# The recurrence's Q projection moves into the stage of half products of a one-layer decoder step

## What is computed

```python
h = rmsnorm(x, lp['norm_mix'])
z = h @ lp['w_in']                      # 1024 x (10*256 + 4*1024)
qa, ka, va, qb, fb, ib, gb, xc, gc, xd, gl = jnp.split(z, split_at, axis=-1)
...
log_f = jnp.logaddexp(jnp.log(lb), jnp.log1p(-lb) + jax.nn.log_sigmoid(fr))
kb = (1.0 - lb) * jax.nn.sigmoid(-fr)
qh = jax.nn.silu(qb.astype(F32))
o, S = gla_chunk_scan(to_h(qh), to_h(kb), to_h(ib.astype(F32)), to_h(log_f), S0.astype(F32), chunk)
o = rmsnorm(o, lp['hgrn_norm']).reshape(B, L, BRANCH_W) * jax.nn.silu(gb.astype(F32))
```

## Time and profile before

| | before |
|---|---|
| median of 3 runs | 1751.24 us |
| the profiled execution, its own time | 1751.34 us |
| its span in the profile | 1749.5 us |
| TensorE busy | 1723.3 us, 98% |
| VectorE, ScalarE, GpSimd busy | 65%, 42%, 45% |
| granted TensorE clock | 0.999 of full speed |
| DMA | 214.80 MB, 123 GB/s in the mean |

### The profile page before, as it was taken

The page is one execution under the profiler, slowest core; times in us unless marked ns, Lnnn a source line. Parts: engine busy times, 40 slices in busy tenths (PEclk is TensorE's granted clock), DMA queues, the critical chain, the costliest instruction groups (busy, mean ns, idle before and its releaser), DMA issues.

```text
span 1749.5 us, 30931 instructions
## 1 busy us (share of the span) xinstructions
PE 1723.3 (98%) x12865; PEld 1676.3 (96%) x12865; DVE 1140.7 (65%) x1275; ACT 733.4 (42%) x1038; POOL 781.6 (45%) x531
## 2 busy tenths in 40 slices
PE   8999999999999999999999999999999999999998
PEld 8999999998999977899999999999999999999998
DVE  6931115826774667657745877888888887775844
ACT  6433334443422556612335554444444443333521
POOL 1666773431222311212123476677776637668021
PEclk9999999999999999999999999999999999999999
DMA  6643226132221542456524222232222375334032
GB/s 229 76 124 117 99 75 215 37 101 81 67 82 68 196 118 67 159 195 236 209 74 148 86 87 105 101 120 99 99 99 99 117 287 209 117 118 148 26 128 95
DMA packets 84798, 214.80 MB, mean 123 GB/s; under 512 B 14866, under 2 KB 32050, under 8 KB 83506
## 3 DMA queue, kind: packets, MB, share of 16 engines
q1 hardware_dynamic: 73714, 189.48, 31.9%
q0 software_dynamic: 4032, 14.68, 2.7%
q10 hardware_dynamic: 6912, 8.65, 1.4%
HBM read 149.48 MB, written 63.40 MB: 122 GB/s over the span
## 4 chain that ended last, share of the span: by engine, by line
PE 91%; DVE 3%; ACT 2%; DMA 2%; issue 1%; POOL 0%; SPq 0%; DVEq 0%; ACTq 0%; POOLq 0%
PE ps L1656 24%; PE ps L1106 21%; PE ps L1704 10%; PE ps L1093 10%; PE ps L1236 10%; PE ps L1688 3%; PE ps L1324 2%; PE ps L1191 1%; DMA masks<-in_wb 1%; PE ps L1409 1%; PE ps L1133 1%; PE ps L1573 1%; PE ps L1443 1%; PE ps L1430 1%; PE ps L1741 1%
## 5 line engine op out<-in xcount | busy, mean ns | idle before, releaser
L3384 POOL TENSOR_TENSOR Wl<-BIG,Wh 128x512 fp32r<-128x512 f32 x110 | 144.0, 1318 | 115.3 <-ACT Wh L2211 115.3
L3241 POOL CAST Uh<-BIG 128x1024 fp32r<-128x1024 f32 x27 | 36.5, 1350 | 283.8 <-PE ps L1093 193.8
L3030 DVE SCALAR_TENSOR_TENSOR ps<-BIG,fpar,ps 128x1023 f32<-128x1023 f32 x84 | 107.9, 1285 | 36.1 <-ACT ps L2302 35.2
L1093 PE MATMUL ps<-Hh,Uh 128*128 128x352 f32 x384 | 127.2, 331 | 0.8 <-ACT BIG L1940 0.8
L2565 DVE TENSOR_TENSOR BIG<-BIG,ps 128x528 f32<-128x528 f32 x45 | 31.6, 704 | 144.2 <-PE ps L1236 143.9
L1093 PE MATMUL ps<-Hh,Ul 128*128 128x352 f32 x384 | 123.5, 322 | 0.0
L1093 PE MATMUL ps<-Hl,Uh 128*128 128x352 f32 x384 | 123.3, 321 | 0.0
L3336 POOL TENSOR_TENSOR Ul<-BIG,Uh 128x1024 fp32r<-128x1024 f32 x15 | 36.1, 2412 | 163.3 <-ACT Uh L2171 163.3
L1656 PE MATMUL ps<-Hl,Wh 128*128 128x264 f32 x528 | 107.1, 284 | 0.0
L3019 DVE TENSOR_TENSOR BIG<-BIG,ps 128x528 f32<-128x528 f32 x110 | 77.3, 703 | 42.8 <-PE ps L1656 36.9
L1704 PE MATMUL ps<-Sl,Vh 128*128 128x264 f32 x504 | 101.9, 283 | 0.0
(11 more groups left out here) (496 smaller groups left out, 5590.6 us busy)
## 6 DMA issues: line engine op xcount, KB each, us to landing
BIG<-in_wu SPq DMA_DIRECT2D x44, 512.0 KB, 4.6
hidden<-BIG SPq DMA_DIRECT2D x22, 528.0 KB, 2.7
late_gates<-BIG SPq DMA_DIRECT2D x18, 528.0 KB, 3.0
BIG<-sums SPq DMA_DIRECT2D x12, 792.0 KB, 4.9
BIG<-in_wgl SPq DMA_DIRECT2D x9, 1024.0 KB, 6.0
BIG<-in_wd SPq DMA_DIRECT2D x6, 1536.0 KB, 9.7
H<-late_gates SPq DMA_DIRECT2D x17, 528.0 KB, 4.4
gates<-BIG ACTq DMA_DIRECT2D x48, 176.0 KB, 1.9
```

What stands on the lines that cost most here:

```text
L1093: ins = nc.tensor.matmul(psb(fill_bank(p)), w[:, u % 2, k], x[:, k, part * PART:part * PART + PART], start=(k == 0 and w is Uh and x is Hh ...
L3030: link(v.scalar_tensor_tensor(y[:, back:SEQ], x[:, 0:SEQ - back], w, y[:, back:SEQ], ALU.mult, ALU.add), v.scalar_tensor_tensor(ys[:, :, b ...
L3384: nc.gpsimd.tensor_tensor(Wl[:, b], src, Wh[:, b].bitcast(F32), ALU.subtract).then_inc(S("w_lo"), 1)
```

## The change

The Q pair is no longer made by `block_z`. It becomes pair number 1 (`Z_PAIR`) of now 10 pairs: its raw weights come from the last two tiles of `wz` (`Z_COLS` has Q's columns last), its sums are made like a gate's, its two rows skip the sigmoid, go to `late_gates`, and SP loads them into `QB` later. `RING` and `USERS` lose QB0 and QB1. Behind the pairs come F, G, then V: FB0 and FB1 take the place of QB0 and QB1, GB0 and GB1 that of FB0 and FB1. TensorE puts the transposes of `turn` around VA0 and between VA0 and VA1. ScalarE's `before()` starts when groups 0 to 3 of the transposes are copied; it loads a table set first, and the copies of groups 4 to 11 and of VA0 and VA1 stand between its steps. The counts of semaphores and the index of a gate in `late_gates` follow. The diff, with one line around each edit:

```diff
@@ -66,7 +66,7 @@
 NORM_ORDER = (KA, KA + 1, QA, QA + 1)
-Z_COLS = (1792, 2304, 2048, 1280, 768, 1024, 1536, 512, 256, 0)
+Z_COLS = (1792, 2304, 2048, 1280, 1024, 1536, 512, 256, 0, 768)
@@ -132,8 +132,8 @@
          "gc_kept0": ("pages_in3", 0), "gc_kept1": ("s0_in", 0), "a_lo": ("vt_done", 12)}
-PAGES_FROM = (32, 80, 80, 32)
-SIG_FROM = (("pages_in0", 288), ("pages_in1", 336), ("pages_in2", 336), ("pages_in3", 288),
+PAGES_FROM = (48, 80, 96, 32)
+SIG_FROM = (("pages_in0", 304), ("pages_in1", 336), ("pages_in2", 352), ("pages_in3", 288),
             ("s0_in", 64), ("cd_in", 128), ("gate_stored0", 384), ("gate_stored1", 384))
@@ -183,9 +183,10 @@
 FILLS = QKS + UNITS
-ZB = 14
+ZB = 12
 COVER = 2
-PAIRS = (4 * LATE - COVER) // 2
+Z_PAIR = 1
+PAIRS = (4 * LATE - COVER) // 2 + 1
 SPLITS = ZB + FILLS
@@ -236,9 +237,9 @@
-USERS = ("XC0", "XC1", "XD0", "XD1", "GC0", "GC1", "IB0", "IB1", "C00", "C01", "QB0", "QB1", "C10", "C11", "FB0", "FB1",
-         "D0", "D1", "GB0", "GB1", "VA0", "VA1")
-RING = ("XD0", "XD1", "GC0", "GC1", "IB0", "IB1", "QB0", "QB1", "FB0", "FB1", "GB0", "GB1", "VA0", "VA1")
+USERS = ("XC0", "XC1", "XD0", "XD1", "GC0", "GC1", "IB0", "IB1", "C00", "C01", "FB0", "FB1", "C10", "C11", "GB0", "GB1",
+         "D0", "D1", "VA0", "VA1")
+RING = ("XD0", "XD1", "GC0", "GC1", "IB0", "IB1", "FB0", "FB1", "GB0", "GB1", "VA0", "VA1")
 FRONT = RING.index("IB1") + 1
@@ -684,7 +685,8 @@
             def pair_weights(c, sem):
-                src = a["wgl"].rearrange("i v p k m -> (i v) p k m")[COVER + 2 * c:COVER + 2 * c + 2]
+                first = COVER + 2 * (c - (c > Z_PAIR))
+                src = a["wz"][18:20] if c == Z_PAIR else a["wgl"].rearrange("i v p k m -> (i v) p k m")[first:first + 2]
                 sp.dma_start(gate_raw(c), src.rearrange("h p k m -> p h k m")).then_inc(on(sem), 16)
@@ -774,6 +776,9 @@
             rows_back(2, Z[:, GC:GC + 2, :], on("gw_in0"))
+            for half in range(2):
+                sp.wait_ge(*upto(f"g_stored{half}", 16 * (Z_PAIR + 1)))
+            sp.dma_start(QB, late_gates[2 * Z_PAIR:2 * Z_PAIR + 2].rearrange("i p t -> p i t")).then_inc(on("gw_first"), 16)
@@ -829,7 +834,8 @@
                 i, u = divmod(s, 8)
-                src = gates[i * EARLY + TURN_OF[u] + QKS] if u < EARLY else late_gates[i * LATE + u - EARLY - COVER]
+                n = i * LATE + u - EARLY - COVER
+                src = gates[i * EARLY + TURN_OF[u] + QKS] if u < EARLY else late_gates[n if n < 2 * Z_PAIR else n + 2]
                 sp.dma_start(gate_row(s), src).then_inc(S(gate_loaded(s)[0]), 16)
@@ -1250,19 +1256,21 @@
             for i in range(2):
-                block_z(f"QB{i}")
+                block_z(f"FB{i}")
             pe.wait_ge(S("cd_in"), 128)
...
             for i in range(2):
-                block_z(f"FB{i}")
+                block_z(f"GB{i}")
             for i in range(2):
                 unit(f"D{i}", wpool[:, i], Z[:, XD + i], 3 + i)
-            turned_v(0, turn[:, 0], range(2))
-            block_z("GB0", (0, lambda: turned_v(0, turn[:, 0], (2,))))
-            turned_v(1, turn[:, 1], range(2))
-            block_z("GB1", (0, lambda: turned_v(1, turn[:, 1], (2,))))
-            block_z("VA0")
+
+            def input_turned():
+                turned_v(0, turn[:, 0], (2,))
+                turned_v(1, turn[:, 1], (0,))
+            turned_v(0, turn[:, 0], (0, 1))
+            block_z("VA0", (0, input_turned))
+            turned_v(1, turn[:, 1], (1, 2))
             block_z("VA1")
@@ -1837,10 +1845,10 @@
-            def turned_v(n):
-
-                for g in range(3):
-                    m = 3 * n + g
+            def turned_out(ms):
+
+                for m in ms:
+                    n, g = divmod(m, 3)
                     act.wait_ge(S("vt_done"), m + 1)
@@ -1867,7 +1875,10 @@
                     act.wait_ge(*upto("g_copied", 2 * c + 2))
-                nc.scalar.activation(GY[:, half], GY[:, half], ACT.Sigmoid).then_inc(on("g_sig"), 1)
+                if c == Z_PAIR:
+                    act.sem_inc(on("g_sig"), 1)
+                else:
+                    nc.scalar.activation(GY[:, half], GY[:, half], ACT.Sigmoid).then_inc(on("g_sig"), 1)
@@ -1921,16 +1932,13 @@
                 for g in range(2):
-                    z_out(("QB", "FB")[i] + str(g), (QB, FB)[i][:, g])
+                    z_out(("FB", "GB")[i] + str(g), (FB, Z[:, GB:GB + 2, :])[i][:, g])
             for i in range(2):
...
             act.wait_ge(S("pool_read"), 2)
-            turned_v(0)
-            z_out("GB0", Z[:, GB, :])
-            turned_v(1)
-            z_out("GB1", Z[:, GB + 1, :])
+            turned_out(range(4))
@@ -1946,14 +1954,16 @@
                 f, q, g = FB[:, 0], QB[:, 0], Z[:, GB, :]
+                act.preload_act_table_set("natural_log_exp_and_others")
                 act.wait_ge(S("d_rows"), 16)
-                for user in ("FB0", "QB0", "GB0"):
+                for user in ("FB0", "GB0", "FB1", "GB1"):
                     z_wait(user)
-                for user in ("FB1", "QB1", "GB1"):
-                    z_wait(user)
+                act.wait_ge(*upto("gw_first", 48))
                 link(nc.scalar.activation(bE, f, ACT.Abs))
...
                 nc.scalar.activation(bE, bE, ACT.Ln, bias=1.0).then_inc(S("b_acts"), 1)
+                turned_out((4, 5))
+                z_out("VA0", turn[:, 0])
                 act.wait_ge(S("b_pre"), 1)
@@ -1963,8 +1973,11 @@
                 chunk_decays()
+                z_out("VA1", turn[:, 1])
+                turned_out((6, 7))
                 act.wait_ge(S("b_pre"), 5)
                 nc.scalar.activation(bE, bd_, ACT.Exp, scale=-1.0).then_inc(S("b_acts"), 1)
+                turned_out(range(8, 12))
@@ -2002,10 +2015,6 @@
                     before()
-                    for j in range(2):
-                        z_out(f"VA{j}", turn[:, j])
-                    for j in range(2):
-                        turned_v(2 + j)
                     act.wait_ge(S("c_rows"), 16)
@@ -2613,7 +2622,7 @@
-            dve.wait_ge(*upto("gw_in1", 80))
+            dve.wait_ge(*upto("gw_in1", 96))
             for i in range(2):
@@ -3240,7 +3249,7 @@
                 pool.wait_ge(S("w_hi"), r_ - 1)
-                if r_ == RING.index("QB1"):
+                if r_ == RING.index("FB1"):
                     pool.wait_ge(*upto("g_stored0", 16 * PAIRS))
```

## The result

The changed kernel takes 1758.37 us in the median (six runs, 1757.47 to 1760.88) against 1751.24 us for the kernel before (now six runs as well, 1749.55 to 1753.83). The ratio on record is 1.0037, with a 95% interval of 1.0026 to 1.0048; the two medians alone give 1.0041. It is slower by about 7 us, where 0.3 us less was forecast, and it lies above the range of 1748.4 to 1752.6. The profiled execution is 1755.7 us long, 6.2 us more than that of before.

The account below looks back on a forecast made before the run. It took TensorE, busy 98% of the span, as the bound: -2.79 us for the products and +2.5 us for later keys gave -0.3 us, 1750.9 us from a median of 1751.24, range 1748.4 to 1752.6.

Parts of the forecast that it names:

- The products and E: Front stage: a 20.58 us pair replaces 23.37 us of blocks, -2.79 us; E, the end of VA1, moves from 397.94 to 395.15.
- Movement through DRAM: Writes to `late_gates`, load into QB and weight loads stay hidden: nothing, with 0 to 0.1 us kept for more traffic.
- the order F, G, V: F, G, V instead of Q, F, G keeps block distances and the transposes' sum: nothing, at most 0.2 us either way.
- ScalarE's chain: Preparation under V, now behind D: spill lands in 6.0 us, first sigmoid at 386.8, eight small multiplications start at 395.1.
- The ports: After E, GpSimd's cast and subtraction hold VectorE's eight small multiplications; keys' transposes at 402.0, E + 6.8 against E + 4.33: +2.5 us.
- TensorE's other condition: All 12 groups of transposes must be copied, until E + 5.0; alone costs 0.7 us, covered by the 2.5 us for the keys.
- The sum: Whole kernel: -2.79 + 2.5 = -0.3 us, from the 1751.24 us median to 1750.9 us.
- the sum's term +2.5: Behind VA1: the keys' transposes start 2.5 us later after E, counted as 2.5 us of the kernel's time.
- a difference behind the state products: Sign of a wrong prediction: any difference arising behind the state products, where it counted none.
- the rivals: Preparation in time, 1749.1 (0.28); shuffle free, 1748.4 to 1747.7 (0.10); late spill, 1751.9 (0.12); pair's late data, 1 to 3 us (0.05).
- rival 3: Pooling rows' spill lands late, at 9.7 us; ScalarE's logs wait, keys end near 402.9: net +0.7 us, 1751.9; chance 0.12.
- The chance of 0.06 for a loss of over 0.2%: Whole kernel slower by over 0.2%, through the pair's weights or rows coming late or a spill landing over 12.5 us.

Follow-up runs that it names:

- experiment 1: Changed kernel with GpSimd's cast and subtraction of the tile behind V held until VectorE has made the keys; 1751.75 us, ratio 0.9996 to the kernel before.
- experiment 2: Changed kernel with 14 more products of 352 columns, used by nothing, where TensorE waits for the keys; 1753.97 us, ratio 1.0009 to the kernel before.
- experiment 6: Changed kernel with half a gate product (12 of 24 products) brought forward into the gap behind VA1, GpSimd's split not held; 1754.00 us, ratio 1.0011 to before.
- experiment 3: Kernel before, with one added wait so VectorE's eight small multiplications come only after VA1 is copied out of PSUM; 1760.06 us, ratio 1.0041.

## Why the prediction was wrong

**The products and E: right.** E came at 395.39, forecast 395.15; 0.20 of the 0.24 stood already at the first pair. A new wait of 0.4 us at FB0 for ScalarE replaced the 0.6 us that TensorE had lost to VectorE in the last pair.

**Movement through DRAM and the order F, G, V: right.** No wait in the changed profile goes back to the rows of Q. The spill landed later than at its 6.0 us, and ScalarE's logs began at 379.17, 1.7 us later than in my sum; that used up room that was there: 1.34 us were left, in which ScalarE idled behind the logs.

**ScalarE's chain: right.** The first sigmoid began at 386.83, forecast 386.8, and the eight multiplications at 395.17, forecast 395.1.

**The ports: right.** The hold of the small form, which no row had shown, is 5.32 us against 2.44 in experiment 1. The Trainium skill's rule ("SBUF — State Buffer", section "Who interferes with whom") and this case agree on it; that the eight run in a two-port mode is what the rule asks for, and no trace shows the mode. For operations with two SBUF inputs that section of the Trainium skill names only GpSimd instructions that read SBUF, which the prediction left out; GpSimd's two here read it. The keys' transposes began at 402.04 (forecast 402.0), released by VectorE's key multiplication, and the state products at 404.17 (forecast 404.0).

**TensorE's other condition: right.** The copies of the 12 groups were forecast to allow the keys at E + 5.0; with the ports free they did so at E + 4.86 (experiment 1).

**The sum: wrong, in the price of the wait.** The step that failed is "What follows is mostly TensorE again, so a shift there should reach the end", and with it the sum's term +2.5: I took 2.5 us of waiting as 2.5 us and put what it does to the work behind it at nothing. That work was priced at the clock of before, whose windows all read 1.00, and I never asked what the longer gap does to that. The runs showed 12 us of products at half speed in its place, about 6 us. In the profiles: -2.55 up to E (-2.79 for the pair, the rest as above), +2.32 from E to the keys' transposes, and +6.4 from there to the end, 5.8 of it up to the first level product; together +6.2 us. The prediction had named this as a sign of being wrong, a difference behind the state products, "where I count none"; the state products themselves started within its bounds. None of the rivals had the clock; rival 3, meant as the one on the slower side, had a mechanism that took place (the late spill) and cost nothing. The chance of 0.06 for a loss of over 0.2% followed from rivals that were all late transfers. The Trainium skill ("TensorE: Matmul & The Clock Gate", section "What's actually happening") says that the clock has a throttled and a full state and that recent activity decides between them; by it a stretch that empties is worth a rival of its own. The traces agree on the two states (0.50 and 1.00) and on activity as the cause (experiment 2: the same gap filled, and 1.00 throughout).

Open: why the clock stayed down for 12 us of full work in the changed kernel and for 3.4 us in experiment 6, and where exactly it falls in the runs of experiment 1 that have no trace.

## What to carry to other kernels

Look up TensorE's busy share and clock in the stretch that a change makes emptier, and price a new wait there twice: once as the wait, once as the work behind it at half clock. If the gap cannot be closed, move independent products into it, even if that gains no time by itself. And where a chain of small VectorE operations moves later, see what GpSimd does at its new place: here one wait on GpSimd gave back 2.9 us of VectorE's time. An execution's own scatter counts as well: up to the first pair, where nothing had been altered, the profiled executions already stood 2.1 us apart (104.91 to 107.03), so a trace is read from a point inside it, such as E, and not from its total.

## What the runs showed of the hardware that I had not expected

A stretch of 6.65 us in which TensorE is busy for 2.72 us, 2.50 us of it idle at the end, stood ahead of the fall of the granted clock from 1.00 to 0.50 in the trace of the changed kernel, and all six of its runs have mean clocks of 0.994 to 0.996; one of 6.37 us with 4.05 us busy had no fall behind it in the trace of before. The clock then stayed at 0.50 through 12 us of unbroken work, and for 17 us in experiment 3. One of 6.91 us with 4.09 us busy (experiment 1) kept it in the traced run, while eight of its eleven runs had a mean below 1.000 and took 1750.6 to 1753.5 us, so one and the same order of work lost clock in some runs and not in others. One of 6.67 us with 4.36 us busy, 2.20 us idle at the end (experiment 6), had a fall of 3.4 us behind it.
